# A hybrid decoder block on one core: all 24 input projections in three rounded products

## The chip, the core and the metric

The kernel runs on one core of a Trainium2 chip. The metric is the device time of one execution in microseconds (us). The core has engines with instruction queues of their own: TensorE (PE in the profile, with its weight loads as PEld), VectorE (DVE), ScalarE (ACT), GpSimd (POOL) and SyncE (SP, which here only starts transfers). Each takes its own instructions strictly one after another; semaphores order the engines among each other.

## The reference

What is computed, cut to what matters here (512 rows of 1024 values, one layer):

```
mod  = silu(c) @ w_ada + b_ada              # 6 vectors: shift, scale, gate for mixer and ffn
h    = rms_norm(x, g_attn) * (1 + sc_a) + sh_a
proj = h @ w_in                             # 1024 x 3072: dq dk dv sq sk sv, 512 columns each
a_out = diff_attention(norm(dq), norm(dk), dv, lam)      # 4 heads, two 64-wide maps each
b_out = stick_breaking_attention(sq, sk, sv)             # 8 heads of 64
x    = x + gt_a * (concat(norm(a_out), norm(b_out)) @ w_out)
h    = rms_norm(x, g_ffn) * (1 + sc_f) + sh_f
x    = x + gt_f * hier_moe(h)               # top group of 4, then top 2 of its 8 SwiGLU experts
```

## The kernel before

Everything is float32. The hidden rows lie transposed in SBUF as `hT` (128 partitions x 8 blocks `k` x 512 rows). The input projection is cut into 24 *jobs* of one PSUM bank (128 x 512) each, summed over the eight blocks `k`: eight `qk` jobs (dq and dk), four `v` jobs with second number 0 (dv), four `sq`, four `sk` and four `v` jobs with second number 1 (sv). `w_in` arrives in six pieces of 512 columns (2 MB) in two buffers, `stage[:, 0]` and `stage[:, 1]`; piece n is loaded once the last job on piece n - 2 is done (L374).

There are two ways to run a job:

- **plain float32** (`run`, L1225): eight matmuls of 128x128 by 128x512, each of which TensorE shows as two passes. Job 0 (`qk` 0) and the twelve jobs `sq`, `sk` and `v` 1 run so, from `hT` and the raw piece.
- **three products** (`run_split`, L1273): each operand is the sum of a rounded high part and a rounded rest (type fp32r), and high x high, high x rest and rest x high are summed, 24 matmuls. Jobs 1 to 11 (`qk` 1 to 7 and `v` 0) run so.

The parts are made ahead of a job. VectorE rounds the rows into `hT_hi` (L827); the rests `hT_lo` are made in turn by VectorE (L830) and GpSimd (L490). A *chunk* of the weights is 128 columns of a piece over all eight blocks. ScalarE rounds it into `w_hi` (`w_round`, L594, in the buffer `work`, which has four chunk places), and VectorE writes the rest over the raw chunk (`w_rest`, L820). In the kernel before, chunks 1 to 11 are split, all in the head of the program.

After the head (the eight `qk` jobs with their norm, the four `v` 0 jobs and the two gate jobs) come 16 *steps*, one for each unit u (head u // 4, query block u % 4) of the differential attention. The lists made by `plan_jobs` set which job runs in which step: one whole job in each of the steps 0 to 7 (`sq` 0 to 3, `sk` 0 to 3), half a job in each of the steps 8 to 15 (`v` 1). In steps 3 and 7 a small job `col` follows, which turns sums of the modulation into columns with 128x1 matmuls; steps 9 and 11 have gate jobs.

What each engine runs in step s, in this order:

- TensorE (L1420): `scores(s)`, `probT_make(s-1)` (transposes the probabilities, L1330, once `prob_ready` of unit s-1 is there), `pv(s-2)`, now and then `fin_T`, then the step's job.
- ScalarE (L693): `job_evac` of the job of step s-1 (waits until that job is done), `probT_evac(s-1)`, `exp_unit(s)`.
- VectorE (L949): `job_evac` (for `col` and gate jobs only), `combine_unit(s-1)` (L911 to L915; gives `prob_ready`), `max_unit(s)` (L900), in steps 0 to 7 `ada_quarter` (two L776-type sums of 128x1024).

After step 15 come the stick-breaking attention, the output projection, the router and the expert loop over 16 pairs of experts, whose weights (96 MB and more) stream through six slots. Slot 0 lies over `hT`.

GpSimd's queue in the head: constants, two transfers for `gates`, then the transfers of the other modulation vectors in quarters of 1 MB (L498). Quarters 0 and 1 wait only for `scale_used`; the rests of the odd blocks `k` stand between quarter 1 and quarter 2. SyncE's queue in the head: x, eight quarters of `w_ada`, piece 0, small parameters, piece 1.

Of the kernel before, what the change touches and what calls it, by code (L numbers as in the profile page):

```python
# [5 lines left out]
F32 = mybir.dt.float32  # L6
# [7 lines left out]
P = 128  # L14
# [30 lines left out]
def plan_jobs():  # L45
# [11 lines left out]
    steps[7].append((("col", 3), None))  # L57
# [43 lines left out]
def hymba_block(nc, x, c, w_ada, b_ada, g_attn, w_in, q_norm_g, k_norm_g, lambda_q1, lambda_k1,  # L101
# [11 lines left out]
    with ExitStack() as ctx:  # L113
# [18 lines left out]
        xr = sb("xr", [P, NT, D])  # L132
        stage = placed_sb("stage", [P, 3, 4096])
        hT = sb("hT", [P, KD, T])
        qkT = placed_sb("qkT", [P, 16, T])
        val = sb("val", [P, NT, 1024])
        mixT = placed_sb("mixT", [P, KD, T])
# [3 lines left out]
        obuf = placed_sb("obuf", [P, 4, T])  # L141
# [13 lines left out]
        hT_hi = rounded("hT_hi", [P, KD, T], "qkT", 8 * T)  # L155
        hT_lo_parts = [rounded("hT_lo0", [P, 4, T], "mixT"), rounded("hT_lo1", [P, 4, T], "obuf")]
        w_hi = rounded("w_hi", [P, KD, 512], "work", 4096)
        w_lo_parts = rounded("w_lo", [P, 2, 4096], "stage")

        def hT_lo(k):  # L160
            return hT_lo_parts[k // 4][:, k % 4, :]
# [80 lines left out]
        wr_ready = sem("wr_ready")  # L242
# [103 lines left out]


# [8 lines left out]
        def _(sp):  # L356
# [40 lines left out]
            sp.wait_ge(job_done, job_no[("v", 3, 1)] + 1)  # L397
            sp.wait_ge(ada_used, 16)
# [42 lines left out]
        def _(pool):  # L441
# [39 lines left out]

            for v in range(GATE_A, GATE_F + 1):
                for i in range(4):
# [3 lines left out]
                    if n == 2:  # L487
                        for k in range(1, KD, 2):
                            pool.wait_ge(hT_hi_ready, k + 1)
                            g.tensor_tensor(hT_lo(k), hT[:, k, :], hT_hi[:, k, :].bitcast(F32),  # L490
                                            ALU.subtract).then_inc(hT_lo_pool, 1)
# [26 lines left out]

            for w in range(2 * NT - 1):
# [44 lines left out]
        def _(act):  # L564
# [29 lines left out]
            def w_round(n):  # L594
                raw, hi, _, arrived, value = split_chunk(n)
                act.wait_ge(arrived, value)
                if n >= 4:
                    act.wait_ge(job_done, n - 3)
# [94 lines left out]
            for s in range(STEPS):  # L693
                if 1 <= s < DIFF_STEPS:
                    for job in step_jobs.get(s - 1, ()):
                        job_evac(job)
                if 1 <= s <= NT * DH:
                    probT_evac(s - 1)
# [63 lines left out]
        def _(dve):  # L762
# [62 lines left out]
            for k in range(KD):  # L825
                dve.wait_ge(hT_raw, k + 1)
                v.tensor_copy(hT_hi[:, k, :], hT[:, k, :]).then_inc(hT_hi_ready, 1)  # L827
                if k % 2 == 0:
                    dve.wait_ge(hT_hi_ready, k + 1)
                    v.tensor_tensor(hT_lo(k), hT[:, k, :], hT_hi[:, k, :].bitcast(F32),  # L830
# [358 lines left out]
        def _(pe):  # L1189
# [35 lines left out]
            def run(job, part=None):  # L1225
# [7 lines left out]
                if kind in ("qk", "sq", "sk"):  # L1233

                    n_in, ch = {"qk": (job[1] // 4, job[1] % 4), "sq": (3, job[1]), "sk": (4, job[1])}[kind]
                    w, arrived, value = piece(n_in)
                    pe.wait_ge(arrived, value)
                    for k in ks:
                        if n == 0:
                            pe.wait_ge(hT_raw, k + 1)  # L1240
                        ins = mm(bank, w[:, k, ch * P:(ch + 1) * P], hT[:, k, :], start=(k == 0), stop=(k == KD - 1))  # L1241
                elif kind == "v":
                    w, arrived, value = piece(2 if job[2] == 0 else 5)
                    pe.wait_ge(arrived, value)
                    for k in ks:
                        ins = mm(bank, hT[:, k, job[1] * P:(job[1] + 1) * P], w[:, k, :], start=(k == 0), stop=(k == KD - 1))  # L1246
# [26 lines left out]
            def run_split(job):  # L1273

                n = job_no[job]
                bank = banks[:, n % 2, :]
                if n >= 2:
                    wait_freed(job_at[n - 2])
                pe.wait_ge(w_split, n if n < 8 else 11)
                if n == 1:  # L1280
                    pe.wait_ge(hT_lo_dve, KD // 2)
                    pe.wait_ge(hT_lo_pool, KD // 2)
                lo = w_lo_parts[:, (2 if n >= 8 else n // 4) % 2, :].rearrange("p (k n) -> p k n", k=KD)
                for k in range(KD):
                    if job[0] == "qk":
                        part = slice((n % 4) * P, (n % 4 + 1) * P)
                        products = [(w_hi[:, k, part], hT_hi[:, k, :]), (w_hi[:, k, part], hT_lo(k)),
                                    (lo[:, k, part], hT_hi[:, k, :])]
                    else:
                        part = slice(job[1] * P, (job[1] + 1) * P)  # L1290
                        products = [(hT_hi[:, k, part], w_hi[:, k, :]), (hT_hi[:, k, part], lo[:, k, :]),
                                    (hT_lo(k)[:, part], w_hi[:, k, :])]
                    for m, (still, moving) in enumerate(products):
                        ins = mm(bank, still, moving, start=(k + m == 0), stop=(k == KD - 1 and m == 2))  # L1294
                ins.then_inc(job_done, 1)

            for i, job in enumerate(head_jobs):
                if i == 0 or job[0] == "gate":
                    run(job)
                else:  # L1300
                    run_split(job)
# [301 lines left out]
```

## Time and profile before

| | us |
|---|---|
| median of 3 runs | 695.13 |
| lowest and highest of these | 694.84, 1225.97 |
| the profiled execution | 697.3 |
| its span in the profile | 695.5 |
| TensorE busy (matmuls) | 574.0 (83% of the span) |
| VectorE busy | 264.1 (38%) |
| ScalarE busy | 166.2 (24%) |
| GpSimd busy | 94.1 (14%) |

The span is cut here by what the program does: the head to 126, the 16 steps of the differential attention to about 260, stick-breaking attention and output projection to about 410, routing to about 430, the expert loop to about 673 (in it the transfers run at 415 GB/s in most slices), and the end. The profile gives the chain of work that ended last: TensorE has 69% of it, transfers 14%, VectorE 6%. Durations of matmuls overlap in the records, since they are pipelined, so what a job takes is best read from the start of its first matmul to the start of what follows; the chain of waits shows just that.

### The profile page before, as it was taken

Reading aid. Unit: us, or ns where it says so; the run is one execution under the profiler, and the core shown is the slowest. Engines: PE = TensorE matmul, PEld = TensorE weight load, DVE = VectorE, ACT = ScalarE, POOL = GpSimd, SP = SyncE. Lnnn points to the kernel's source line nnn. Section 1 sums busy time; section 2 is a strip of 40 time slices with the busy share of each in tenths; the row PEclk is TensorE's granted clock in tenths of the full one; section 3 lists DMA queues with packets and bytes.
Section 4 is the critical chain, followed back from the end, with each engine's and each line's share of the span. In section 5 each row is a group of like instructions: output and inputs, shape, how many; then the busy total and the mean of one; then the engine's idle time right before and its main releaser. Section 6 shows DMA issues by size and latency. Waiting matters only on the chain.

```text
span 695.5 us, 7423 instructions
## 1 busy us (share of the span) xinstructions
PE 574.0 (83%) x2904; PEld 347.1 (50%) x2904; DVE 264.1 (38%) x446; ACT 166.2 (24%) x286; POOL 94.1 (14%) x126
## 2 busy tenths in 40 slices
PE   3389989999989897999999952899899988788740
PEld 2247768445454454777744632555445544344320
DVE  3866670553734363132212245332224223132005
ACT  7044541121222245655204220000000000000002
POOL 8230110000000001111103201112112111110000
PEclk9999999998998998999999985899999999899985
DMA  9984762536130007000093065599999999999819
GB/s 346 407 277 135 289 215 101 181 124 239 61 122 0 1 4 299 0 1 1 1 398 145 31 256 230 186 403 417 416 416 416 415 416 416 417 416 417 367 53 354
DMA packets 42385, 163.25 MB, mean 235 GB/s; under 512 B 7796, under 2 KB 7796, under 8 KB 34164
## 3 DMA queue, kind: packets, MB, share of 16 engines
q1 hardware_dynamic: 31972, 134.52, 48.6%
q0 software_dynamic: 9248, 26.23, 10.7%
q10 hardware_dynamic: 1136, 2.11, 0.8%
q8 instruction: 19, 0.31, 0.2%
q14 instruction: 10, 0.08, 0.0%
HBM read 158.64 MB, written 12.58 MB: 246 GB/s over the span
## 4 chain that ended last, share of the span: by engine, by line
PE 69%; DMA 14%; DVE 6%; SPq 6%; ACT 2%; issue 2%; POOL 0%; POOLq 0%; DVEq 0%
PE banks L1523 11%; PE banks L1241 10%; PE banks L1294 8%; PE banks L1415 8%; PE banks L1542 6%; PE banks L1381 6%; PE banks L1246 4%; DMA stage<-in_w_in_dram 4%; DMA obuf<-in_w_dram 4%; DMA qkT<-in_w_dram 3%; PE banks L1393 3%; PE banks L1370 2%; PE banks L1511 2%; DMA stage<-pair_rows 2%; SPq L359 1%
## 5 line engine op out<-in xcount | busy, mean ns | idle before, releaser
L1241 PE MATMUL banks<-hT,stage 128*128 128x512 f32 x144 | 67.4, 623 | 1.5 <-DMA stage<-in_w_in_dram 1.5
L1542 PE MATMUL banks<-stage,work 128*64 128x512 f32 x168 | 60.9, 632 | 8.8 <-ACT work L744 6.3
L1523 PE MATMUL banks<-qkT,work 128*64 128x256 f32 x272 | 61.8, 384 | 0.8 <-DMA stage<-in_w_dram 0.8
L742 ACT ACTIVATE work<-banks 128x256 f32<-128x256 f32 x16 | 6.1, 384 | 221.0 <-PE banks L1523 221.0
L1415 PE MATMUL banks<-stage,mixT 128*128 128x512 f32 x128 | 56.1, 594 | 0.0
L1146 DVE TENSOR_TENSOR work<-banks,gates 128x1024 f32<-128x1024 f32 x16 | 19.6, 1225 | 82.2 <-PE banks L1542 82.2
L776 DVE SCALAR_TENSOR_TENSOR mixT<-stage,small,mixT 128x1024 f32<-128x1024 f32 x35 | 44.9, 1282 | 3.5 <-DMA stage<-in_w_ada_dram 2.8
L1241 PEld LDWEIGHTS banks<-hT,stage 128*128 128x128 f32 x144 | 28.3, 202 | 34.6 <-issue 32.0
L1523 PE MATMUL banks<-hT,work 128*64 128x256 f32 x192 | 43.5, 384 | 2.5 <-DMA qkT<-in_w_dram 2.5
L535 POOL DMA_INDIRECT pair_rows<-work,tables x16 | 16.1, 1005 | 198.8 <-DVE work L1146 198.8
L1381 PE MATMUL banks<-work,consts 128*128 128x128 f32 (+3 forms) x160 | 39.2, 402 | 2.9 <-POOL work L507 2.9
L1141 DVE TENSOR_TENSOR work<-work,banks 128x256 f32<-128x256 f32 x16 | 6.7, 422 | 88.1 <-ACT work L742 88.1
L1523 PEld LDWEIGHTS banks<-qkT,work 128*64 128x64 f32 x272 | 36.6, 138 | 6.3 <-issue 1.7
L1523 PE MATMUL banks<-mixT,work 128*64 128x256 f32 x160 | 36.0, 381 | 3.1 <-DMA obuf<-in_w_dram 2.4
L1415 PEld LDWEIGHTS banks<-stage,mixT 128*128 128x128 f32 x128 | 23.9, 190 | 27.7 <-issue 27.7
L1523 PE MATMUL banks<-stage,work 128*64 128x256 f32 x160 | 35.8, 381 | 0.0
L1381 PEld LDWEIGHTS banks<-work,consts 128*128 128x128 f32 x160 | 27.3, 199 | 15.7 <-issue 7.3
L1523 PEld LDWEIGHTS banks<-hT,work 128*64 128x64 f32 x192 | 26.0, 139 | 17.6 <-issue 3.7
L1542 PEld LDWEIGHTS banks<-stage,work 128*64 128x64 f32 x168 | 17.5, 144 | 31.6 <-issue 24.6
L1246 PE MATMUL banks<-stage,hT 128*128 128x512 f32 x64 | 31.0, 630 | 0.0
L946 DVE SCALAR_TENSOR_TENSOR work<-banks,work 128x1280 f32<-128x1280 f32 x8 | 11.9, 1492 | 48.3 <-ACT work L685 48.2
L1523 PEld LDWEIGHTS banks<-mixT,work 128*64 128x64 f32 x160 | 21.3, 137 | 14.7 <-DMA obuf<-in_w_dram 3.3
(242 smaller groups left out, 1044.4 us busy)
## 6 DMA issues: line engine op xcount, KB each, us to landing
stage<-in_w_dram SPq DMA_DIRECT2D x31, 1024.0 KB, 21.0
qkT<-in_w_dram SPq DMA_DIRECT2D x23, 1024.0 KB, 21.3
stage<-in_w_ada_dram POOLq DMA_DIRECT2D x16, 1024.0 KB, 5.6
stage<-in_w_in_dram SPq DMA_DIRECT2D x6, 2048.0 KB, 9.8
hT<-in_w_dram SPq DMA_DIRECT2D x12, 1024.0 KB, 18.4
val<-in_w_dram SPq DMA_DIRECT2D x10, 1024.0 KB, 18.7
mixT<-in_w_dram SPq DMA_DIRECT2D x10, 1024.0 KB, 19.6
alibi<-in_w_dram SPq DMA_DIRECT2D x5, 1024.0 KB, 24.1
```

Source lines behind the costliest of these rows:

```text
L535: g.indirect_dma_start(y_dram, bass.IndirectOffsetOnAxis(ap=tables[:, 1, q:q + 1], axis=0), ysb[:, r, :], None, bounds_check=2 * T - 1, oo ...
L776: return v.scalar_tensor_tensor(out=dst, in0=src, scalar=s, in1=dst, op0=ALU.mult, op1=ALU.add)
L1146: v.tensor_tensor(ysb[:, r, :], banks[:, 4 + 2 * r:6 + 2 * r, :].rearrange("p b k -> p (b k)"), gates[:, 1, :], ALU.mult).then_inc(ysb_rea ...
L1241: ins = mm(bank, w[:, k, ch * P:(ch + 1) * P], hT[:, k, :], start=(k == 0), stop=(k == KD - 1))
L1246: ins = mm(bank, hT[:, k, job[1] * P:(job[1] + 1) * P], w[:, k, :], start=(k == 0), stop=(k == KD - 1))
L1294: ins = mm(bank, still, moving, start=(k + m == 0), stop=(k == KD - 1 and m == 2))
L1370: ins = mm(zps[n % 2][:, ZOFF[kb]:ZOFF[kb] + W], k, q, start=(kb != 3), stop=True, skip_group_check=True)
L1381: ins = mm(zps[n % 2][:, o:o + W], negtri if j == kb else negones, soft[:, n % 2, ZOFF[j]:ZOFF[j] + W], start=False, stop=True, skip_group ...
L1393: ins = mm(banks[:, 7, i * P + s * HD:i * P + (s + 1) * HD], stick[:, n % 2, o:o + P], val[:, kb, 512 + n * HD:512 + (n + 1) * HD], start= ...
L1415: ins = mm(banks[:, w % 5, :], mixT[:, k, t * P:(t + 1) * P], wv[:, k % 4, half * 512:(half + 1) * 512], start=(k == 0), stop=(k == KD - 1))
L1523: ins = mm(banks[half * C:(half + 1) * C, 2, up * F:(up + 1) * F], heT[:, r, k * P + half * C:k * P + (half + 1) * C], ws[2 * place + half ...
L1542: ins = mm(banks[half * C:(half + 1) * C, 4 + 2 * r + col, :], geT[:, fc * P + half * C:fc * P + (half + 1) * C], w2s[2 * place + half][:, ...
```

## The change

All 24 jobs run as three products, through one new function `project`. `run_split` is gone.

- Job 0 becomes three products too, in two sweeps: high x high and rest x high as each `hT_hi` block arrives, and then, when all rests are there, high x rest. Its chunk, chunk 0, is split by GpSimd: a cast and a subtraction, put ahead of the quarters.
- Chunks 12 to 23 are split inside the steps: `split_at(s)` says that step 0 splits chunks 12 and 13, steps 1 to 6 one chunk each (s + 13), step 7 the chunks 20, 21 and 22, step 8 chunk 23. On ScalarE `w_round` stands behind `job_evac` of the step before and ahead of `probT_evac`; on VectorE `w_rest` stands behind `job_evac` and ahead of `combine_unit`.
- `hT_hi` must now live until the last `v` job. It lies over `xr` (x), and the rests are written over `hT` itself. So x is loaded a second time (2 MB) after the last projection, ahead of expert 0, and GpSimd waits for it before it adds the mixer's output.
- `col` 3 moves from the end of step 7 to the start of step 8's list, ahead of the first half of `v` 1.

```diff
-    steps[7].append((("col", 3), None))
+    steps[8].insert(0, (("col", 3), None))
...
-        hT_hi = rounded("hT_hi", [P, KD, T], "qkT", 8 * T)
-        hT_lo_parts = [rounded("hT_lo0", [P, 4, T], "mixT"), rounded("hT_lo1", [P, 4, T], "obuf")]
+        hT_hi = rounded("hT_hi", [P, KD, T], "xr")
+        hT_lo = rounded("hT_lo", [P, KD, T], "hT")
...
+        def split_at(s):
+
+            return {0: (12, 13), 7: (20, 21, 22), 8: (23,)}.get(s, (s + 13,) if s < 7 else ())
+
+        IN_JOBS = ([("qk", n) for n in range(8)] + [("v", t, 0) for t in range(NT)] + [("sq", n) for n in range(4)]
+                   + [("sk", n) for n in range(4)] + [("v", t, 1) for t in range(NT)])
+
+        def chunk_job(n):
+
+            return IN_JOBS[n // 4 * 4 + 3] if IN_JOBS[n][0] == "v" else IN_JOBS[n]
...
             sp.wait_ge(job_done, job_no[("v", 3, 1)] + 1)
+            sp.dma_start(xr[:], x_rows).then_inc(x_again, 16)
...
+            raw, hi, lo, arrived, value = split_chunk(0)
+            pool.wait_ge(arrived, value)
+            g.tensor_copy(hi, raw).then_inc(w0_hi, 1)
+            pool.wait_ge(w0_hi, 1)
+            g.tensor_tensor(lo, raw, hi.bitcast(F32), ALU.subtract).then_inc(w0_split, 1)
...
+            pool.wait_ge(x_again, 16)
             for w in range(2 * NT - 1):
...
                 if n >= 4:
-                    act.wait_ge(job_done, n - 3)
+                    act.wait_ge(job_done, job_no[chunk_job(n - 4)] + 1)
                 a.activation(hi, raw, ACT.Copy).then_inc(w_hi_ready, 1)
...
                     for job in step_jobs.get(s - 1, ()):
                         job_evac(job)
+                for n in split_at(s):
+                    w_round(n)
                 if 1 <= s <= NT * DH:
                     probT_evac(s - 1)
...
                     for job in step_jobs.get(s - 1, ()):
                         job_evac(job)
+                for n in split_at(s):
+                    w_rest(n)
                 if 1 <= s <= NT * DH:
                     combine_unit(s - 1)
...
+            def project(job, bank, ks):
+
+                c = IN_JOBS.index(job)
+                lo = w_lo_parts[:, c // 4 % 2, :].rearrange("p (k n) -> p k n", k=KD)
+                if job[0] == "v":
+                    pe.wait_ge(w_split, c // 4 * 4 + 3)
+                    part = slice(job[1] * P, (job[1] + 1) * P)
+                    for k in ks:
+                        mm(bank, hT_hi[:, k, part], w_hi[:, k, :], start=(k == 0), stop=False)
+                        mm(bank, hT_hi[:, k, part], lo[:, k, :], start=False, stop=False)
+                        ins = mm(bank, hT_lo[:, k, part], w_hi[:, k, :], start=False, stop=(k == KD - 1))
+                    return ins
+                part = slice((c % 4) * P, (c % 4 + 1) * P)
+                if c == 0:
+
+                    pe.wait_ge(w0_split, 1)
+                    for k in ks:
+                        pe.wait_ge(hT_hi_ready, k + 1)
+                        mm(bank, w_hi[:, k, part], hT_hi[:, k, :], start=(k == 0), stop=False)
+                        mm(bank, lo[:, k, part], hT_hi[:, k, :], start=False, stop=False)
                     pe.wait_ge(hT_lo_dve, KD // 2)
                     pe.wait_ge(hT_lo_pool, KD // 2)
...
+                    for k in ks:
+                        ins = mm(bank, w_hi[:, k, part], hT_lo[:, k, :], start=False, stop=(k == KD - 1))
+                    return ins
+                pe.wait_ge(w_split, c)
+                for k in ks:
+                    mm(bank, w_hi[:, k, part], hT_hi[:, k, :], start=(k == 0), stop=False)
+                    mm(bank, w_hi[:, k, part], hT_lo[:, k, :], start=False, stop=False)
+                    ins = mm(bank, lo[:, k, part], hT_hi[:, k, :], start=False, stop=(k == KD - 1))
+                return ins
```

Three places in the engines' order. The first is VectorE at the seam of steps 0 and 1: from the end of step 0 (the sums on `mixT` are `ada_quarter`) through `combine_unit(0)` (RECIPROCAL to the write of `work`) to the first instruction of `max_unit(1)`. Before:

```order
L775 TENSOR_SCALAR mixT<-stage,small 128x1024 [waits quarter_in0,job_done]
L776 SCALAR_TENSOR_TENSOR mixT<-stage,small,mixT 128x1024 [waits dve_chain]
L911 RECIPROCAL small<-small 128x2 [waits exp_ready,ada_used]
L912 TENSOR_SCALAR small<-small 128x1 [waits dve_chain]
L914 TENSOR_SCALAR work<-work,small 128x128 [waits dve_chain]
L915 SCALAR_TENSOR_TENSOR work<-work,small 128x128 [waits dve_chain]
L900 ISA work,small<-banks,alibi 128x256 [waits score_done]
```

Of the change (its lines are numbered anew: L841 is `w_rest`, L929 to L933 `combine_unit`, L918 `max_unit`):

```order
L793 TENSOR_SCALAR mixT<-stage,small 128x1024 [waits quarter_in0,job_done]
L794 SCALAR_TENSOR_TENSOR mixT<-stage,small,mixT 128x1024 [waits dve_chain]
L841 TENSOR_TENSOR w_lo<-stage,w_hi 128x8x128 [waits w_hi_ready,ada_used]
L929 RECIPROCAL small<-small 128x2 [waits exp_ready]
L930 TENSOR_SCALAR small<-small 128x1 [waits dve_chain]
L932 TENSOR_SCALAR work<-work,small 128x128 [waits dve_chain]
L933 SCALAR_TENSOR_TENSOR work<-work,small 128x128 [waits dve_chain]
L918 ISA work,small<-banks,alibi 128x256 [waits score_done]
```

The rest of a chunk, which waits for ScalarE's rounding, now stands ahead of the combination.

The second place is ScalarE in steps 0 to 2: `exp_unit` (two instructions), the evacuation of the finished job into `qkT`, `probT_evac` (`work<-banks`). Before:

```order
L654 ACTIVATE work,small<-work,small 128x128 [waits max_ready]
L654 ACTIVATE work,small<-work,small 128x128
L631 ACTIVATE qkT<-banks 128x512 [waits job_done]
L662 ACTIVATE work<-banks 128x128 [waits T_done]
L654 ACTIVATE work,small<-work,small 128x256 [waits max_ready]
L654 ACTIVATE work,small<-work,small 128x256
L631 ACTIVATE qkT<-banks 128x512 [waits job_done]
L662 ACTIVATE work<-banks 128x256 [waits T_done]
```

Of the change (L615 is `w_round`, L647 the evacuation):

```order
L615 ACTIVATE w_hi<-stage 128x8x128 [waits job_done,piece_in1] x2
L670 ACTIVATE work,small<-work,small 128x128 [waits max_ready]
L670 ACTIVATE work,small<-work,small 128x128
L647 ACTIVATE qkT<-banks 128x512 [waits job_done]
L615 ACTIVATE w_hi<-stage 128x8x128 [waits job_done,piece_in1]
L678 ACTIVATE work<-banks 128x128 [waits T_done]
L670 ACTIVATE work,small<-work,small 128x256 [waits max_ready]
L670 ACTIVATE work,small<-work,small 128x256
L647 ACTIVATE qkT<-banks 128x512 [waits job_done]
L615 ACTIVATE w_hi<-stage 128x8x128 [waits job_done,piece_in1]
```

Each rounding stands directly behind the evacuation of the job of the step before.

The third place is GpSimd in the head, from the transfers for `gates` to the copies for the router. Before:

```order
L480 DMA gates<-in_b_ada_dram 128x1024 x2
L498 DMA stage<-in_w_ada_dram 128x2x1024 [waits scale_used]
L498 DMA stage<-in_w_ada_dram 128x2x1024
L490 TENSOR_TENSOR hT_lo_50<-hT,hT_hi 128x512 [waits hT_hi_ready] x2
L490 TENSOR_TENSOR hT_lo_51<-hT,hT_hi 128x512 [waits hT_hi_ready] x2
L493 COPY wr<-wrA 128x8x4 [waits params_in]
```

Of the change:

```order
L489 DMA gates<-in_b_ada_dram 128x1024 x2
L493 CAST w_hi<-stage 128x8x128 [waits piece_in0]
L495 TENSOR_TENSOR w_lo<-stage,w_hi 128x8x128 [waits w0_hi]
L513 DMA stage<-in_w_ada_dram 128x2x1024 [waits scale_used]
L513 DMA stage<-in_w_ada_dram 128x2x1024
L505 TENSOR_TENSOR hT_lo<-hT,hT_hi 128x512 [waits hT_hi_ready] x4
L508 COPY wr<-wrA 128x8x4 [waits params_in]
```

The two quarters' transfers and GpSimd's four rests now stand behind the wait for piece 0 and the split of chunk 0.

## Rows read from the trace of the kernel before

**Rows 1.** The page, part 4: shares of the chain that ended last, by engine.
```profile
PE 69%; DMA 14%; DVE 6%; SPq 6%; ACT 2%; issue 2%; POOL 0%; POOLq 0%; DVEq 0%
```

**Rows 2.** The chain that ended last, from 59 to 233: start us, us, what.
```profile
59.16 5.49 PE banks L1294 x24
...
99.45 7.34 PE banks L1294 x24
...
126.24 7.06 PE banks L1241 x16
133.31 0.63 PE banks L1316 x4
...
134.20 6.87 PE banks L1241 x16
...
149.37 1.06 PE banks L1316 x4
...
229.63 3.44 PE banks L1246 x8
```

**Rows 3.** VectorE and ScalarE at steps 0 and 1: start, us, instruction [idle before].
```profile
125.93 0.69 DVE L871 TENSOR_TENSOR gates<-banks,gates 128x512 f32<-128x512 f32 x1 [0.26 <-PE banks L1251]
...
133.34 0.60 ACT L631 ACTIVATE qkT<-banks 128x512 f32<-128x512 f32 x1 [5.19 <-PE banks L1241]
...
137.51 0.17 DVE L911 RECIPROCAL small<-small 128x2 f32<-128x2 f32 x1
...
138.35 0.48 DVE L915 SCALAR_TENSOR_TENSOR work<-work,small 128x256 f32<-128x256 f32 x1
```

**Rows 4.** Lines L599 (rounds a chunk) and L823 (its rest): ns min/median/max, starts.
```profile
L599 ACT ACTIVATE w_hi<-stage x11: 1045/1049/1093, 44.7 to 96.5; 128x1024 fp32r<-128x1024 f32 x11
...
L823 DVE TENSOR_TENSOR w_lo<-stage,w_hi x11: 1210/1224/1226, 48.7 to 98.1; 128x1024 fp32r<-128x1024 f32 x11
```

**Rows 5.** The same chain where a col job (L1256) ends a step.
```profile
158.23 3.58 PE banks L1256 x16
...
162.10 0.18 DVE small L911
...
163.88 1.11 PE banks L1330 x4
...
166.27 7.85 PE banks L1241 x16
...
200.80 3.58 PE banks L1256 x16
...
207.02 1.11 PE banks L1330 x4
```

**Rows 6.** Windows: us, busy of PE, PEld, DVE, ACT, POOL, PEclk, DMA share, GB/s.
```profile
97.00:99.40 2.40, 0.24 (x1) 0.00 (x0) 2.30 (x3) 2.37 (x5) 0.00 (x0) 1.00 0.75 208
99.40:103.00 3.60, 3.55 (x9) 2.86 (x10) 3.11 (x3) 0.35 (x1) 0.00 (x0) 0.56 1.03 401
```

**Rows 7.** TensorE's transpositions after two waits on VectorE, in order of time.
```profile
222.70 0.44 PE L1330 MATMUL banks<-consts,work 128*128 128x128 f32 x2 [0.72 <-DVE work L915]
...
236.41 1.12 PE L1330 MATMUL banks<-consts,work 128*128 128x128 f32 x4 [2.06 <-DVE work L915]
```

**Rows 8.** The head in order of time: GpSimd, and the start of job 0.
```profile
5.52 1.49 POOL L464 TENSOR_SCALAR alibi<-work 128x512 f32<-128x512 int32 x1
...
13.05 0.97 POOL L469 CAST consts<-work 128x128 f32<-128x128 int32 x1
...
27.74 1.44 POOL L498 DMA_DIRECT2D stage<-in_w_ada_dram  x2 [7.01 <-DVE mixT L776]
...
41.82 1.37 POOL L490 TENSOR_TENSOR hT_lo<-hT,hT_hi 128x512 fp32r<-128x512 f32 x1 [12.64 <-DVE hT_hi L827]
...
42.80 10.03 PE L1241 MATMUL banks<-hT,stage 128*128 128x512 f32 x16 [1.49 <-DMA stage<-in_w_in_dram]
...
48.83 2.18 POOL L490 TENSOR_TENSOR hT_lo<-hT,hT_hi 128x512 fp32r<-128x512 f32 x1 [0.96 <-DVE hT_hi L827]
```

More of the change, by code:

```diff
@@ L129, in sem @@
             return ctx.enter_context(nc.semaphore(name))
-        xr = sb("xr", [P, NT, D])
+        xr = placed_sb("xr", [P, NT, D])
         stage = placed_sb("stage", [P, 3, 4096])
-        hT = sb("hT", [P, KD, T])
-        qkT = placed_sb("qkT", [P, 16, T])
+        hT = placed_sb("hT", [P, KD, T])
+        qkT = sb("qkT", [P, 16, T])
         val = sb("val", [P, NT, 1024])
-        mixT = placed_sb("mixT", [P, KD, T])
+        mixT = sb("mixT", [P, KD, T])
         gates = sb("gates", [P, 2, D])
@@ L140, in hymba_block @@
         work = placed_sb("work", [P, 8192])
-        obuf = placed_sb("obuf", [P, 4, T])
+        obuf = sb("obuf", [P, 4, T])
         consts = sb("consts", [P, 6, P])
@@ L151, in hymba_block @@
         plan = sb("plan", [1, 2 * NQOV + 2], I32)
-        hT_hi = rounded("hT_hi", [P, KD, T], "qkT", 8 * T)
-        hT_lo_parts = [rounded("hT_lo0", [P, 4, T], "mixT"), rounded("hT_lo1", [P, 4, T], "obuf")]
+        hT_hi = rounded("hT_hi", [P, KD, T], "xr")
+        hT_lo = rounded("hT_lo", [P, KD, T], "hT")
         w_hi = rounded("w_hi", [P, KD, 512], "work", 4096)
         w_lo_parts = rounded("w_lo", [P, 2, 4096], "stage")
-        def hT_lo(k):
-            return hT_lo_parts[k // 4][:, k % 4, :]
         ident, negtri, negones, ones, halves, slot_iota = (consts[:, n, :] for n in range(6))
@@ L241, in hymba_block @@
         c_in, params_in, gate_bias_in = sem("c_in"), sem("params_in"), sem("gate_bias_in")
-        wr_ready = sem("wr_ready")
+        wr_ready, x_again, w0_hi, w0_split = sem("wr_ready"), sem("x_again"), sem("w0_hi"), sem("w0_split")
         first_in = [sem(f"first_in{n}") for n in range(8)]
@@ L489, in _ @@
                             pool.wait_ge(hT_hi_ready, k + 1)
-                            g.tensor_tensor(hT_lo(k), hT[:, k, :], hT_hi[:, k, :].bitcast(F32),
+                            g.tensor_tensor(hT_lo[:, k, :], hT[:, k, :], hT_hi[:, k, :].bitcast(F32),
                                             ALU.subtract).then_inc(hT_lo_pool, 1)
@@ L829, in _ @@
                     dve.wait_ge(hT_hi_ready, k + 1)
-                    v.tensor_tensor(hT_lo(k), hT[:, k, :], hT_hi[:, k, :].bitcast(F32),
+                    v.tensor_tensor(hT_lo[:, k, :], hT[:, k, :], hT_hi[:, k, :].bitcast(F32),
                                     ALU.subtract).then_inc(hT_lo_dve, 1)
@@ L1232, in run @@
                 kind = job[0]
[L1233 to L1246, printed above, removed]
+                if kind in ("qk", "sq", "sk", "v"):
+                    ins = project(job, bank, ks)
                 elif kind == "gate":
@@ L1271, in qk_norm @@
                 mm(banks[:, 2 + n % 2, :], halves, sqb[:, n % 2, :], start=True, stop=True).then_inc(norm_done, 1)
[L1273 to L1280, printed above, removed]
+            def project(job, bank, ks):
[16 more added lines that the diff above has]
+                        mm(bank, lo[:, k, part], hT_hi[:, k, :], start=False, stop=False)
@@ L1281, in run_split @@
                     pe.wait_ge(hT_lo_dve, KD // 2)
                     pe.wait_ge(hT_lo_pool, KD // 2)
[L1283 to L1294, printed above, removed]
@@ L1295, in run_split @@
-                ins.then_inc(job_done, 1)
+                    for k in ks:
[6 more added lines that the diff above has]
+                    ins = mm(bank, lo[:, k, part], hT_hi[:, k, :], start=False, stop=(k == KD - 1))
@@ L1297, in _ @@
+                return ins
             for i, job in enumerate(head_jobs):
[L1298 to L1301, printed above, removed]
+                run(job)
                 if 1 <= i <= 8:
```

## The prediction, made before the changed kernel ran

> **What bounds the kernel now.** I read the page's chain that ended last first: TensorE carries 69% of it [rows 1]. Then the same chain in order of time over the head and the 16 steps. The reader is to see there that job follows job almost without a gap: a step is `scores`, a few transpositions and products, and the job. So time taken from a job shortens the program, and time in which TensorE waits lengthens it, as long as nothing else is late. Nothing behind the steps takes such a shift up: the stick-breaking attention, the output projection and the router follow one another, and the expert stream starts from them. Third, I read the other engines in the steps, because the change puts new work into their queues, and the granted clock around TensorE's waits.
>
> **What the products give back.** A plain job takes 6.87 us from its first matmul to what follows, half of one 3.44, and a job of three products 5.49 (24 matmuls, 0.229 each) [rows 2]. That is 1.38 less for each. Twelve jobs (`sq`, `sk`, `v` 1) change so: 12 x 1.38 = 16.6 us gained. Job 0 is costed apart, since it waits for its operands.
>
> The Trainium skill, "TensorE: Matmul & The Clock Gate", section "Back-to-back issue gap", gives about 131 ns for each matmul of 512 columns in a sustained stream of weight loads and matmuls. By it a job of 24 would take 3.1 us and the twelve would give 45. The rows decide: 5.49 for each such job here, so the sum keeps 16.6.
>
> **What the splits in the steps cost.** This is the term that decides. ScalarE needs 1.05 us to round a chunk and VectorE 1.22 for the rest [rows 4]; twelve of each are added, 13 and 15 us, on engines that are idle for more than half of the steps. As mere work they would be hidden. But where they stand is the trouble. In step s (1 to 8) ScalarE rounds behind `job_evac`, which waits until the job of step s - 1 is done. VectorE's rest waits for that rounding, and it stands ahead of `combine_unit(s-1)`, for which TensorE waits before its transpositions and thus before its next job. Before, this combination lay in the shadow of the job: at step 1 it ran from 137.51 to 138.83 [rows 3], while the job lasted until 141.07 [rows 2]. Now it can't start before the job has ended.
>
> The chain from the end t0 of a job: the evacuation starts 0.03 later and takes 0.60 [rows 2, 3]; rounding 1.05, rest 1.22 [rows 4]; so the combination starts at t0 + 2.9. It takes 1.3 us for 256 columns [rows 3] and 1.8 for 512, from 162.10 to TensorE's 163.88 [rows 5]; I take 1.1 for 128 and 1.6 for 384. TensorE's own work meanwhile is only `scores`, 0.63 for 256 columns to 1.06 for 512 [rows 2]; before, it went on right behind that. The added wait is then:
>
> - steps 1, 2, 3, 5, 6: 4.0 - 0.63, 4.2 - 0.85, 4.5 - 1.06 and again the first two, about 3.4 each: 17.0
> - step 7 has three chunks; VectorE, the slower of the two, adds 2 x 1.22: 5.8
> - step 4: `col` 2 ends step 3, and VectorE waits for it already. From the col's end at 161.81 the transpositions started at 163.88 [rows 5]. ScalarE's part is hidden behind the col, so only one rest is added: 1.2
> - step 8: `col` 3 is gone from the end of step 7. Before, 2.6 passed from its end at 204.38 to the transpositions at 207.02 [rows 5]; now 2.9 + 1.8 = 4.7 from the job's end: 2.1. The col itself only moves.
> - step 0: `sq` 0 needs chunk 12. VectorE comes to it after the second gate, at 126.62 [rows 3], and ends at 127.9, against the job's start at 126.24 [rows 2]: 1.7
>
> Together 27.8 us. The bounds: if the engines overlap instructions a little better, 3.0 a step instead of 3.4 (25); if a semaphore takes 0.1 more at each of four hand-overs, 31. In steps 9 to 15 nothing stands in the way; chunk 16 and later find their place in `w_hi` and their piece in time, since both are free steps before.
>
> **What the waits do to the clock.** At 97.0 to 99.4 TensorE was idle and the granted clock still 1.00; from 99.4 to 103.0 it was 0.56, that is mostly 1.2 GHz [rows 6], and the job in it took 7.34 instead of 5.49 [rows 2]: 1.85 lost after 2.2 us of waiting. After 2.06 us of waiting four transpositions took 1.12, so the clock was low there too; after 0.72 two took 0.44 and it was not [rows 7]. The six waits of 3.4 and 5.8 us lie beyond the longer of these, so each brings about 1.85: 11.1. Step 0 with 1.7 lies between; I take half, 0.9. At steps 4 and 8 the clock fell before already (the job at 166.27 took 7.85 [rows 5]). Together 12.0, between 0 (it never falls) and twice as much.
>
> The skill's same page, section "A second HAM failure mode: psum-queue depth-cycling", describes a kernel in which short idle spells between groups of matmuls make the clock go to and fro, so that throughput falls although a matmul at full clock is as fast as ever. The 1.85 us at 99.45 agrees. By that rule this change would pay at every step; without it the sum would be 12 us smaller.
>
> **The head.** Piece 0, landed at 42.80, was what job 0 waited for [rows 8]. Quarters 0 and 1 (2 MB, issued at 27.74 [rows 8]) now come after it; at the 401 GB/s of a full stretch [rows 6] that brings piece 0 forward by 5.2, to 37.6. Then GpSimd casts chunk 0. No row has this operation: its 128x512 from int32 takes 1.49, and a cast of 128x128 0.97 [rows 8], so 128x1024 lies between 1.6 (a fixed cost and little more) and 7.8 (eight times 0.97); I take 3.0, twice the nearest row. The subtraction is twice the 1.37 of 128x512 [rows 8]: 2.7. That makes 43.3, and 44.8 after the quarters' 1.44. Three rests take until 48.9, and the last, which cannot start before 48.83 anyway, again 2.18: 51.1 instead of 51.0. Job 0's last eight products follow in 1.8 at full clock, 52.9, or 3.7 at half, 54.8, against its end before at 52.83. So it gives nothing: plus 1.0, between 0 and 2, and up to 7 if the cast takes 7.8. The quarters land before VectorE wants the first at 53.
>
> **At no cost:** the second x (2 MB, 5.2 us of transfers) falls in the stretch where TensorE works on the last steps and the stick-breaking attention, and expert 0, which it delays, is wanted only in the expert loop at about 430; without that cover it would cost 5. GpSimd waits for it only before the output projection's sums, some 100 us later.
>
> **Sum.** 27.8 + 12.0 + 1.0 - 16.6 = 24.2. On the profiled execution of 697.3 that gives 721.5; the median of the runs is 2.2 below it, so 719.3.
>
> **The rivals.**
>
> - *The waits come, the clock holds.* 697.3 + 27.8 + 1.0 - 16.6 - 2.2 = 707.3. For it: each wait is followed by a long job, and 0.72 did no harm. Against: 2.06 and 2.2 did [rows 6, 7]. 13%.
> - *The clock does not recover in the steps.* The eight jobs of the steps 0 to 7 at half clock lose 5.5 each, 44 instead of 12: about 751. Against: after 99.45 it came back within the job. 6%.
> - *Faster: the rests are hidden.* If rounding and rest of a chunk ended before the job of the step before, the combination would stay where it is in time and only the gain were left: 697.3 + 1.0 - 16.6 - 2.2 = 679.5. It decides at the place of one instruction on each of two engines; any chunk from 13 to 15 needs nothing of the job it queues behind. But the queues are strict, and ScalarE's evacuation waits for the job. 4%.
> - *The products run at the skill's 131 ns*, from the sentence above: with the waits, 28 less than the forecast, 691. The rows stand against it. 1%.
> - The change doing something else than it says: 1%.
>
> **How the numbers follow.** The forecast has 75%; its own range is 712 to 731 (waits 25 to 31, clock 6 to 20, head 0 to 7, not all at one end). The range reaches down to the rival with the steady clock and up part of the way to the one without recovery: 706 to 738. A change of 2% is 13.9 us, about what a measurement can tell from none: above 709 is slower, below 681 faster. Slower is the forecast, the third of the rival at 707 that would end above 709, and 6%: about 83%; faster 4%; the rest, 13%, within 2%.
>
> **What would show it.** In the profile after: jobs of 5.5 us in the steps; on VectorE the rests of chunks 14 to 19 starting 1.7 after each job's end and the RECIPROCAL right behind; TensorE idle for 3.4 us ahead of the transpositions, released by L933 (the combination), and about 5.8 in step 7; a granted clock near 0.5 behind each. Job 0 ends near 53 to 55. From the stick-breaking attention on, every stretch has its old length. I am wrong if VectorE's combination starts before the job's end, or if TensorE's wait is seen to be much shorter than 3 us.

## The result

The changed kernel takes 724.0 us (median of 4 runs, 720.5 to 726.6), the kernel before 695.5: a ratio of 1.040, with a 95% interval of 1.036 to 1.044. (The kernel before has three runs from 694.8 to 695.8 and one of 1226.0, which the ratio leaves out.) It is slower, as forecast; 719.3 was predicted, in a range of 706 to 738.

The page of the profile after has the same parts as that of before. Its first part, the clock's line of the second, and the first line of the fourth, which answers [rows 1]:

```profile
span 724.7 us, 7670 instructions
...
PE 572.4 (79%) x3008; PEld 378.6 (52%) x3008; DVE 279.0 (38%) x458; ACT 177.5 (24%) x298; POOL 97.4 (13%) x128
...
PEclk9999999879678799999999996599999999989985
...
PE 65%; DMA 12%; DVE 11%; SPq 5%; ACT 4%; issue 2%; POOL 0%; DVEq 0%; POOLq 0%; ACTq 0%
```

The span grew by 29.2 us, but TensorE is busy no longer than before (572.4 against 574.0). VectorE and ScalarE gained 15 and 11 us of work, and their shares of the chain rose from 6% to 11% and from 2% to 4%. The clock's digits sag to 8, 7 and 6 in slices 8 to 14, which are the steps 0 to 8; only slice 10, which is step 3 and the `col` job behind it, keeps its 9.

Three stretches, from the chains of both profiles, show where the time went: the head up to the first gate job (124.01 before, 128.48 after) grew by 4.5; the steps up to the first matmul of the stick-breaking attention (260.28, 290.12) grew from 136.3 to 161.6, by 25.4; all that follows takes 434.6 instead of 435.2, so it is the same.

Step 1 after, in order of time, answers [rows 3] (start, us, instruction, idle time before it and what ended it):

```profile
139.62 0.70 PE L1329 MATMUL banks<-qkT 64*128 64x256 f32 x4
139.73 0.60 ACT L647 ACTIVATE qkT<-banks 128x512 f32<-128x512 f32 x1 [4.84 <-PE banks L1310]
140.22 1.05 ACT L615 ACTIVATE w_hi<-stage 128x1024 fp32r<-128x1024 f32 x1
141.37 1.23 DVE L841 TENSOR_TENSOR w_lo<-stage,w_hi 128x1024 fp32r<-128x1024 f32 x1 [5.40 <-ACT w_hi L615]
142.51 0.16 DVE L929 RECIPROCAL small<-small 128x2 f32<-128x2 f32 x1
...
143.28 0.35 DVE L933 SCALAR_TENSOR_TENSOR work<-work,small 128x128 f32<-128x128 f32 x1
...
143.68 0.47 PE L1343 MATMUL banks<-consts,work 128*128 128x128 f32 x1 [3.36 <-DVE work L933]
```

The reader sees the whole mechanism in seven lines. The job of step 0 ends at 139.6; evacuation, rounding, rest and combination follow one another; TensorE has only `scores` to do and then waits 3.36 us. VectorE had been idle for 5.40 us ahead of the rest: it had time for the combination, but the rest stood in front of it.

### The profile page after: what moved, and what is told of

Read it like the earlier page. It is cut to its first block, busy times and chain, and to the rows that moved or that the text cites. A ratio compares the mean times of both kernels' runs of the same rounds, so it can differ in the third digit from the quotient of the medians.

```text
span 724.7 us, 7670 instructions
## 1 busy us (share of the span) xinstructions
PE 572.4 (79%) x3008; PEld 378.6 (52%) x3008; DVE 279.0 (38%) x458; ACT 177.5 (24%) x298; POOL 97.4 (13%) x128
## 4 chain that ended last, share of the span: by engine, by line
PE 65%; DMA 12%; DVE 11%; SPq 5%; ACT 4%; issue 2%; POOL 0%; DVEq 0%; POOLq 0%; ACTq 0%
PE banks L1536 11%; PE banks L1428 8%; PE banks L1555 6%; PE banks L1394 5%; PE banks L1308 4%; PE banks L1309 4%; PE banks L1310 4%; DMA obuf<-in_w_dram 3%; DMA qkT<-in_w_dram 3%; DMA stage<-in_w_ada_dram 3%; PE banks L1406 2%; DVE w_lo L841 2%; PE banks L1383 2%; PE banks L1289 2%; PE banks L1290 2%
## 5 line engine op out<-in xcount | busy, mean ns | idle before, releaser
L1308 PE MATMUL banks<-hT_hi,w_hi 128*128 128x512 f32 x120 | 55.5, 462 | 1.7 <-DVE w_lo L841 1.7
L1309 PE MATMUL banks<-hT_lo,w_hi 128*128 128x512 f32 x120 | 51.9, 432 | 0.0
L1310 PE MATMUL banks<-hT_hi,w_lo 128*128 128x512 f32 x120 | 51.2, 427 | 0.0
L841 DVE TENSOR_TENSOR w_lo<-stage,w_hi 128x1024 fp32r<-128x1024 f32 x23 | 27.7, 1222 | 47.1 <-ACT w_hi L615 46.8
L1428 PEld LDWEIGHTS banks<-stage,mixT 128*128 128x128 f32 x128 | 23.9, 190 | 27.7 <-issue 27.7
L1343 PE MATMUL banks<-consts,work 128*128 128x128 f32 x40 | 9.5, 343 | 32.4 <-DVE work L933 32.4
## 6 DMA issues: line engine op xcount, KB each, us to landing
stage<-in_w_in_dram SPq DMA_DIRECT2D x6, 2048.0 KB, 11.1
hT<-in_w_dram SPq DMA_DIRECT2D x12, 1024.0 KB, 16.6
```

The source lines that it names most:

```text
L841: v.tensor_tensor(lo, raw, hi.bitcast(F32), ALU.subtract).then_inc(w_split, 1)
L1308: mm(bank, w_hi[:, k, part], hT_hi[:, k, :], start=(k == 0), stop=False)
L1309: mm(bank, w_hi[:, k, part], hT_lo[:, k, :], start=False, stop=False)
L1310: ins = mm(bank, lo[:, k, part], hT_hi[:, k, :], start=False, stop=(k == KD - 1))
L1428: ins = mm(banks[:, w % 5, :], mixT[:, k, t * P:(t + 1) * P], wv[:, k % 4, half * 512:(half + 1) * 512], start=(k == 0), stop=(k == KD - 1))
```

## The experiments

Two theories were tested. **Place**: the time is lost because rounding and rest queue behind one thing and ahead of another, and the clock falls in the waits. **Work**: it is lost because ScalarE and VectorE have more to do, or because the products are slower in the steps than they were in the head.

### Only VectorE's place changed

The instructions are those of the changed kernel. VectorE makes the rests behind `max_unit`; only chunk 12 stays in front, since the job of step 0 needs it.

```diff
-                for n in split_at(s):
-                    w_rest(n)
+                if s == 0:
+                    w_rest(12)
                 if 1 <= s <= NT * DH:
                     combine_unit(s - 1)
                 if s < NT * DH:
                     max_unit(s)
+                for n in split_at(s):
+                    if n != 12:
+                        w_rest(n)
```

> The changed kernel, but VectorE makes the rests of the chunks 13 to 23 behind max_unit of their step instead of ahead of combine_unit; the same instructions, only their place differs. If the place is the cause (my theory), the combinations lie in the shadow of the jobs again: of 32.4 us that TensorE waited for L933 about 6 stay, as before the change, and the clock losses of the steps go; 724 - 26 - 12 = about 686, below the kernel before by 9. If the added work on VectorE and ScalarE, or slower products, were the cause (rival), nothing would change: 720 to 726.

Measured: 685.4 us, ratio to the kernel before 0.984 (0.981 to 0.987). The change of place alone turns 4% slower into 1.6% faster. Who waited for whom on TensorE in the steps (us in all, times, longest), first the changed kernel, then this one:

```profile
PE banks L1343 <- DVE work L933: 32.4, 11, 5.5
PE banks L1308 <- DVE w_lo L841: 1.7, 1, 1.7
```

```profile
PE banks L1346 <- DVE work L933: 5.2, 5, 2.1
...
PE banks L1368 <- ACT work L678: 2.5, 3, 2.0
PE banks L1311 <- DVE w_lo L841: 1.7, 1, 1.7
```

The kernel before waited 6.4 us there. So the rival *Work* falls: all the added work is still done, and what it costs is a few us of late transpositions (2.5 at L1368, behind the three roundings of step 7).

### Only ScalarE's place changed

```diff
+                for n in split_at(s):
+                    w_round(n)
                 if 1 <= s < DIFF_STEPS:
                     for job in step_jobs.get(s - 1, ()):
                         job_evac(job)
-                for n in split_at(s):
-                    w_round(n)
```

> The changed kernel, but ScalarE rounds a step's chunks ahead of the evacuation of the job of the step before, so without waiting for it; VectorE's order stays as in the change. Theory: the rests of chunks 14 to 19 are then done during the job before, and steps 1, 2, 3, 5 and 6 lose their wait (17 us) with the clock loss behind it (about 10). Step 4 (the rest queues behind the col's evacuation), step 7 (chunk 22 needs the job of step 6) and step 8 keep theirs: 724 - 17 - 2.4 - 9.3 = about 695. If VectorE's place alone mattered, whatever ScalarE does: no change, 724. If ScalarE's order alone mattered: as low as 686.

Measured: 694.3 us (ratio 0.998, 0.996 to 1.000), as *Place* said for each step apart. The same wait in this kernel's profile:

```profile
PE banks L1343 <- DVE work L933: 14.9, 7, 3.7
```

What it leaves is the waits of steps 4, 7 and 8, where the chunk needs the job just ended or the rest queues behind the col, and those of the gates, as before. It also leaves 2.3 us in step 6, which was not expected: there ScalarE comes to the rounding only after two small instructions for the output norm (L683, L684), and these wait for VectorE's sums:

```profile
180.11 0.30 ACT L683 ACTIVATE small<-small 128x4 f32<-128x4 f32 x1 [3.58 <-DVE small L950]
...
181.63 1.22 DVE L841 TENSOR_TENSOR w_lo<-stage,w_hi 128x1024 fp32r<-128x1024 f32 x1 [1.55 <-ACT w_hi L615]
...
184.14 0.44 PE L1343 MATMUL banks<-consts,work 128*128 128x128 f32 x2 [2.30 <-DVE work L933]
```

So either change of place is enough by itself to free the steps 1, 2, 3 and 5: the wait there needs both, ScalarE behind the job and VectorE ahead of the combination. In steps 4 and 6 only VectorE's place does it (in `rest_behind` step 6 keeps 0.7, and step 4 the 1.4 it had before).

### The wait kept, TensorE kept busy

Useless products run where TensorE waits. They add work to the kernel and take none away.

```diff
                     scores(s)
+                if s in (1, 2, 3, 5, 6, 7):
+                    nj = job_no[step_parts[s][0][0]]
+                    wait_freed(job_at[nj - 2])
+                    for i in range(21 if s == 7 else 13):
+                        mm(banks[:, nj % 2, :], hT_hi[:, i % KD, 0:P], hT_hi[:, i % KD, :], start=True, stop=True)
```

> The changed kernel with useless fp32r products of 128x128 by 128x512 behind scores in the steps 1, 2, 3, 5, 6 (13 each, about 3.0 us) and 7 (21, about 4.8 us), written to the bank that the next job clears; the wait for VectorE stays. It adds work to TensorE only where it waits. If the clock falls because TensorE waits, and that costs about 14 us in the steps (theory), it holds now at those six places: 724 - 11 = about 713, and the granted clock there is 1.00. If the products of three parts are slow in the steps for another reason (operands, banks), the time stays at 724 or grows.

Measured: 713.3 us (ratio 1.025, 1.021 to 1.028), 10.7 less than the changed kernel. Two windows over steps 1 and 2 (us, busy time of PE, PEld, DVE, ACT, POOL, then the granted clock, DMA share, GB/s), first the changed kernel, then this one:

```profile
140.00:148.00 8.00, 4.64 (x15) 3.45 (x12) 5.48 (x12) 2.63 (x7) 0.67 (x1) 0.68 0.12 48
152.00:160.00 8.00, 4.65 (x17) 3.23 (x16) 5.84 (x12) 3.23 (x7) 0.00 (x0) 0.79 0.01 4
```

```profile
140.00:148.00 8.00, 7.82 (x35) 6.14 (x34) 5.48 (x12) 1.83 (x6) 0.71 (x1) 1.00 0.04 10
152.00:160.00 8.00, 7.84 (x36) 5.40 (x34) 4.40 (x9) 2.64 (x7) 0.71 (x1) 1.00 0.22 61
```

With no other difference the granted clock stays at 1.00 and the kernel gets 10.7 us shorter, so that much of the loss was the clock's, about 1.8 for each of the six waits on average. The products themselves are as fast in the steps as in the head once the clock is up: the jobs of these six steps take 5.47 to 5.52.

The average hides a spread. Between the two profiles the steps 1, 2, 3, 5, 6 and 7 get shorter by 2.8, 1.6, 0.0, 2.7, 2.7 and 1.5 us, 11.3 together. In the changed kernel, waits of almost the same length were followed by very different stretches; the job of step 1 took 8.16 and that of step 3 took 5.48, as if there had been no wait. The waits of the two steps, and windows over the start and the end of the one job and over the whole of the other:

```profile
143.68 0.47 PE L1343 MATMUL banks<-consts,work 128*128 128x128 f32 x1 [3.36 <-DVE work L933]
168.64 0.55 PE L1343 MATMUL banks<-consts,work 128*128 128x128 f32 x3 [3.33 <-DVE work L933]
```

```profile
143.70:149.70 6.00, 6.00 (x15) 4.75 (x16) 3.25 (x7) 1.37 (x5) 0.72 (x1) 0.50 0.16 27
149.70:152.20 2.50, 2.50 (x12) 1.80 (x10) 0.00 (x0) 0.00 (x0) 0.00 (x0) 0.99 0.87 352
169.60:175.10 5.50, 5.50 (x27) 4.58 (x25) 2.84 (x5) 1.64 (x5) 0.72 (x1) 1.00 0.14 29
```

No run here shows why step 3 was spared.

### The splits without the products

The kernel before, its jobs plain, with rounding and rest at the change's places. Its results go nowhere. The first pair of lines stands on ScalarE ahead of `probT_evac`, the last on VectorE ahead of `combine_unit`; those between write the rest over the rounded chunk.

```diff
+                for n in split_at(s):
+                    w_round(n)
...
                 raw, hi, lo, _, _ = split_chunk(n)
+                if n >= 12:
+                    lo = hi
...
+                for n in split_at(s):
+                    w_rest(n)
```

> The kernel before, with plain jobs, plus the splits of the chunks 12 to 23 at the very places of the change on ScalarE and VectorE; the rest is written over the rounded chunk, and nobody uses either. It isolates what the splits' places cost without what the products give. Theory: the waits of 26 us in steps 1 to 8 and 11 to 14 for the clock come, the gain and the head's loss don't: 695 + 26 + 12 = about 733 (step 0 waits for nothing here). Rival (the three products themselves or the head lose the time): 695 to 700.

Measured: 731.3 us (ratio 1.050, 1.048 to 1.053). The chain at step 1 reads the same with plain jobs in place of products (start, us, what):

```profile
133.43 1.06 ACT w_hi L610
...
134.58 1.23 DVE w_hi L838
...
136.90 0.48 PE banks L1347
137.37 8.24 PE banks L1258 x16
```

Plain jobs, the old head, and still 36 us lost: the splits at these places cost this by themselves. The changed kernel with its gain and its head stands 7.3 below. The job behind the wait took 8.24 instead of 6.87 [rows 2], which is the clock again (granted 0.64 in its first 3.6 us).

### The head: who splits chunk 0

In the changed kernel the head lost more than was forecast. Its rows around the split, which answer [rows 8]:

```profile
37.77 1.04 POOL L493 CAST w_hi<-stage 128x1024 fp32r<-128x1024 f32 x1 [16.98 <-DMA stage<-in_w_in_dram]
...
38.89 2.34 POOL L495 TENSOR_TENSOR w_lo<-stage,w_hi 128x1024 fp32r<-128x1024 f32 x1
38.94 0.17 DVE L833 TENSOR_TENSOR small<-banks,small 128x8 f32<-128x8 f32 x1 [4.16 <-PE banks L1223]
...
39.21 2.04 DVE L835 SCALAR_TENSOR_TENSOR small<-small 128x8 f32<-128x8 f32 x1
...
41.29 5.46 ACT L607 ACTIVATE hT<-banks,small 128x512 f32<-128x512 f32 x8 [23.97 <-DVE small L835]
...
53.14 3.75 PE L1304 MATMUL banks<-hT_lo,w_hi 128*128 128x512 f32 x8 [1.12 <-POOL hT_lo L505]
```

The last instruction of the modulation, 8 elements wide, took 2.04 us and ended with GpSimd's subtraction; ScalarE's first `hT` block hangs on it. Two runs tried this, both on the kernel of the first experiment. One gives the chunk to ScalarE, ahead of its wait for `mod_a`, and to VectorE, behind its last instruction of the modulation:

```diff
             pool.wait_ge(arrived, value)
-            g.tensor_copy(hi, raw).then_inc(w0_hi, 1)
-            pool.wait_ge(w0_hi, 1)
-            g.tensor_tensor(lo, raw, hi.bitcast(F32), ALU.subtract).then_inc(w0_split, 1)
...
+            a.activation(hi, raw, ACT.Copy).then_inc(w0_hi, 1) 
...
+            v.tensor_tensor(lo, raw, hi.bitcast(F32), ALU.subtract).then_inc(w0_split, 1)
```

> rest_behind, and chunk 0 is rounded by ScalarE ahead of its wait for the modulation and its rest made by VectorE behind it; GpSimd splits nothing and only waits for piece 0 before it starts the quarters. In the changed kernel VectorE's last instruction of the modulation (L835, 128x8) took 2.04 us instead of 0.17 while GpSimd's subtraction ran from 38.89 to 41.23, and ScalarE's first hT came 1.9 later. Theory: GpSimd's two-input subtraction holds VectorE up; without it job 0 ends 2 us sooner, at about 54.8: 685.4 - 2 = 683.4. Rival: the head's 4 us come from job 0's form alone (it waits for the rests, then runs at the low clock): 685.

The other only delays GpSimd's subtraction:

```diff
             pool.wait_ge(w0_hi, 1)
+            pool.wait_ge(mod_a, 1)
```

> rest_behind, but GpSimd waits for mod_a (the end of VectorE's modulation) before it subtracts for chunk 0; the rest as it is. It keeps GpSimd's work and changes only when it runs. Theory (the two engines hold each other up): L835 takes 0.2 again and ScalarE starts hT at about 39.4; but the subtraction now lies beside VectorE's first rest and delays job 0's start to about 41.8 and the quarters' transfers; job 0 ends 1 to 2 us sooner: 684. Rival (L835's 2 us are a wait of another kind, not GpSimd): L835 stays at 2 us, the subtraction only comes later: 686 or more.

Measured: 683.1 us for the first (ratio 0.982, 0.981 to 0.984), against 685.4 for its base, which ran on another chip with the same time of the kernel before. That is the 2 us that were expected, but the runs of the two overlap (681.3 to 684.1, 682.9 to 687.2). The second takes 687.2, but its runs scatter from 682.0 to 688.4, so in the total it is inconclusive. The profiles decide on the instruction, first of `act_head`, then of `sub_late`:

```profile
38.90 0.17 DVE L835 SCALAR_TENSOR_TENSOR small<-small 128x8 f32<-128x8 f32 x1
...
40.25 0.42 DVE L848 CAST hT_hi<-hT 128x512 fp32r<-128x512 f32 x1
```

```profile
39.07 0.17 DVE L836 SCALAR_TENSOR_TENSOR small<-small 128x8 f32<-128x8 f32 x1
...
39.39 2.35 POOL L496 TENSOR_TENSOR w_lo<-stage,w_hi 128x1024 fp32r<-128x1024 f32 x1 [0.77 <-DVE small L836]
...
40.15 1.88 DVE L846 CAST hT_hi<-hT 128x512 fp32r<-128x512 f32 x1 [0.91 <-ACT hT L608]
```

The 2.04 us are gone in both. In `sub_late` GpSimd's work is unchanged and only half a microsecond later, so it was its subtraction that held VectorE up. It now holds up another instruction, VectorE's first rounding of `hT`: 1.88 us instead of 0.42, until 0.3 us behind the end of the subtraction. So `sub_late` keeps little of what it wins; job 0's last eight products start at 52.6, against 53.2 in the base. In `act_head` they start at 51.2. That is the 2 us. The rest of the head's loss is the clock of these eight products, and it comes and goes: they took 3.75 in the changed kernel (granted clock 0.50), 3.59 in `act_head` (0.54) and 2.08 in the base (1.00), so that in the profiles job 0 of `act_head` ends only 0.5 before that of its base.

### The second load of x

The base is the kernel of the first experiment; GpSimd waits for all three loads.

```diff
-            sp.dma_start(xr[:], x_rows).then_inc(x_again, 16)
+            for i in range(3):
+                sp.dma_start(xr[:], x_rows).then_inc(x_again, 16)
+                sp.wait_ge(x_again, 16 * (i + 1))
```

> rest_behind, with x loaded three times instead of once after the last projection (4 MB more, one after another, ahead of expert 0). The prediction put one load at nothing because the transfers are idle there and expert 0 is wanted late. Theory: 685.4, no difference, since 10 us more of transfers still end before expert 0 is wanted. Rival (the load is on the path, or the expert's load behind it is): about 10 us more, 695.

Measured: 686.3 us (684.2 to 686.9) against 685.4 (682.9 to 687.2) with one load. Two further loads cost nothing that can be seen beside the scatter of the runs; the 10 us of the rival are out, so one load costs nothing that matters either.

### All together

`act_head`, both places changed, the chunks spread over the steps so that none has three, and the rest of chunk 12 between the two gates:

```diff
-            return {0: (12, 13), 7: (20, 21, 22), 8: (23,)}.get(s, (s + 13,) if s < 7 else ())
+            return {0: (12, 13), 1: (14, 15), 2: (16,), 3: (17,), 4: (18, 19), 6: (20,), 7: (21, 22), 8: (23,)}.get(s, ())
```

> act_head and round_ahead together on rest_behind, with the chunks spread so that no step has three (steps 0 to 8: 12 13, 14 15, 16, 17, 18 19, none, 20, 21 22, 23), and the rest of chunk 12 ahead of the second gate's evacuation. In rest_behind's trace 2.0 us of fin_T's wait in step 7 (three roundings ahead of the evacuation of the transposed probabilities), 2 us of a late combination in step 6 and step 0's 1.7 are left: 683.4 - 2 - 2 - 0.8 = about 679. If these waits are replaced by others on the same loaded VectorE, 683.

Measured: 682.0 us (ratio 0.982, 0.980 to 0.983), the lowest of all, but its runs (681.6 to 684.4) overlap those of `act_head` (681.3 to 684.1). The 4 us that I expected between them are not there. Its waits on TensorE in the steps:

```profile
PE banks L1349 <- DVE work L938: 5.8, 6, 2.1
...
PE banks L1314 <- DVE w_lo L841: 0.7, 1, 0.7
PE banks L1371 <- ACT work L678: 0.7, 3, 0.2
```

The waits for ScalarE (2.5 to 0.7) and for chunk 12 (1.7 to 0.7) went as meant. The wait for VectorE did not (5.5 to 5.8): the 0.7 of step 6 are gone, but the combination now comes late by 0.6 in step 2 and by 0.4 in step 8, each time behind a step with two rests. This is the case that the expectation named as "replaced by others on the same loaded VectorE". So 2.5 us of waits are saved against `act_head`; in the two profiles the clock took most of that back, since the half job of step 8 took 5.23 (granted clock 0.52) against 2.87 (1.00).

## Why the prediction was right

**The products' gain**, 16.6: a job of products kept its 5.49 at full clock (5.47 to 5.50 in steps 1, 2, 3 and 6 of `rest_behind`), and that run confirms the term as a whole. Its span is 10.1 below that of the kernel before; with what its profile shows against it, 2.4 in the head, 1.7 of step 0's wait and 1.6 more than before of low clock in step 0's job (7.31), the gain comes to 15.8, smaller terms left out.

**The waits**, forecast 27.8: TensorE waited 32.4 for the combination instead of 6.4 and 1.7 for chunk 12, that is 27.7 more. It holds term by term too: steps 1, 2, 3, 5 and 6 have 16.7 (17.0 forecast), step 7 has 5.5 (5.8), step 4 has 1.4 (1.2), step 8 has 1.9 (2.1), step 0 has 1.7 (1.7), and 0.4 more came behind step 15, where none was forecast. In step 1 the transpositions began 4.1 after the job's end, where 4.0 was worked out. Both remedies (`rest_behind`, `round_ahead`) keep every instruction and lose most of these waits, so they come from the place and not from the amount of work.

**The clock**, forecast 12.0: the steps grew by 25.4, and 25.4 - 27.7 + 16.6 leaves 14.3 in the profile, which caught the slowest of the four runs. At the six places with long waits 11.1 was forecast; `filled` gives back 10.7 by the medians and 11.3 there by the profiles. The mechanism is right and the sum too, but the price of 1.85 for each wait holds only on average (0.0 to 2.8), so that the sum came out as close as this is partly luck. Step 0, taken as half a price, 0.9, lost 1.7 more than before: its job took 7.34 instead of 5.49, where the plain job had taken 7.06 instead of 6.87 [rows 2]. The remaining 1.3 lie in steps 4 and 8 to 15, where the kernel before had some low clock already; they are not divided further. Of the rivals, the steady clock (707) is out by `filled`; the one without recovery (751) by the profile, where the clock is back before each job ends (0.99 from 149.70 on in step 1).

**The head**, forecast 1.0 within 0 to 7: job 0 ended at 56.9 instead of 52.8, so 4.1, and with two products of job 1 at low clock it is 4.5 up to the first gate job. This term was mis-sized. Piece 0 came at 37.8 as worked out (37.6), and GpSimd was even quicker than assumed: the cast took 1.04, below even my lower bound (I took 3.0, between 1.6 and 7.8), and the subtraction 2.34, where I took 2.7. What the step left out is VectorE: I asked what GpSimd's work would delay on GpSimd, not what it would do to an instruction of VectorE that happened to run at the same time. That is 1.9 of the 4.1; another 1.9 are the eight last products at half clock, which the text gave as the upper of its two cases and the sum took as half. The range of 0 to 7 held the result, but its upper end was set by a slow cast, which did not come. The trace of the kernel before could have warned of it. There VectorE makes four rests of 128x512, the first with GpSimd idle (0.69) and three beside a subtraction of GpSimd (1.63):

```profile
L830 DVE TENSOR_TENSOR hT_lo<-hT,hT_hi x4: 691/1634/1643, 40.7 to 46.8; 128x512 fp32r<-128x512 f32 x4
```

**At no cost**: the second x. `x_more` agrees. All behind the steps kept its length to 0.6 us.

The 131 ns for a matmul of 512 columns, from the Trainium skill's "TensorE: Matmul & The Clock Gate", section "Back-to-back issue gap", did not show: 0.229 held. Against the 29.2 us of the profile 24.2 were forecast; of the difference 3.5 are the head and 2.3 the clock, and what follows the steps took 0.6 less.

## What to carry to other kernels

When work is added to an engine that is idle most of the time, ask where in its queue it stands: what it waits for, and who waits for what stands behind it. Twelve roundings and twelve subtractions cost 38.6 us at one place (724.0 against 685.4) and about nothing a few instructions further on. ScalarE's place alone would have been a remedy for three quarters of it (694.3). Work that is needed a step later belongs behind what is needed now. Price a wait of TensorE with the clock in it: here a wait of 3.4 us cost 5.2 on average, and from 3.3 to 6.2 one by one.

## What the runs showed of the hardware

- A subtraction of GpSimd on two SBUF operands (128x1024, 2.34 us) stretched a VectorE instruction of 8 elements from 0.17 to 2.04 us, and in `sub_late` a cast of 128x512 from 0.42 to 1.88. L833 and L834, which read PSUM and one SBUF operand, were not touched beside it (0.17 and 0.15). The Trainium skill's "GPSIMD Engine Reference", section "Specifications", says that the SBUF interfaces are shared with VectorE and names instructions with two SBUF inputs; L835 is one, so this trace agrees. The cast has a single SBUF input; the section also names a 2-port performance mode, and no row here shows whether the cast ran in it.
- GpSimd's cast of 128x1024 from float32 to fp32r took 1.04 us, while its cast of 128x8 from int32 had taken 1.17 earlier in the same program: the one can't be scaled from the other.
- The time at low clock behind equal waits differs. In the changed kernel the job behind a wait of 3.3 to 3.4 us took 8.16, 6.68, 5.48, 7.20 and 7.77 us in steps 1, 2, 3, 5 and 6. It also differs between runs: behind a wait of 1.12 us the eight last products of job 0 took 3.75 us in the profile of the changed kernel and 2.08 in that of `rest_behind`, whose head has the same instructions.
